# Sums of the stick-breaking attention: suffix sums of the key blocks on VectorE, a triangle and its complement on TensorE

## What is computed

```python
def block(args):
    qblk, qp = args
    z = jnp.einsum('bhqd,bhkd->bhqk', qblk, kh).astype(jnp.float32) * scale
    strict = kpos[None, :] < qp[:, None]
    log_beta = jax.nn.log_sigmoid(z)
    log_keep = jnp.where(strict, jax.nn.log_sigmoid(-z), 0.0)
    between = lax.cumsum(log_keep, axis=log_keep.ndim - 1, reverse=True) - log_keep
    w = jnp.where(strict, jnp.exp(log_beta + between), 0.0)
    return jnp.einsum('bhqk,bhkd->bhqd', w.astype(vh.dtype), vh)
```

## Time and profile before

| | us |
|---|---|
| time before, median of 3 runs | 2716.53 (2716.38 to 2717.42) |
| the profiled execution's own time | 2714.51 |
| its span | 2712.7 |
| TensorE busy | 2689.5 (99%) |
| VectorE busy | 1578.0 (58%) |
| ScalarE busy | 1152.4 (42%) |
| GpSimd busy | 625.4 (23%) |

### The profile page before, as it was taken

The page is one execution under the profiler, slowest core; times in us unless marked ns, Lnnn a source line. Parts: engine busy times, 40 slices in busy tenths (PEclk is TensorE's granted clock), DMA queues, the critical chain, the costliest instruction groups (busy, mean ns, idle before and its releaser), DMA issues.

```text
span 2712.7 us, 31969 instructions
## 1 busy us (share of the span) xinstructions
PE 2689.5 (99%) x12918; PEld 2252.7 (83%) x12918; DVE 1578.0 (58%) x2312; ACT 1152.4 (42%) x1836; POOL 625.4 (23%) x401
## 2 busy tenths in 40 slices
PE   8999999999999999999999999999999999999999
PEld 7888888888888888888888888788888888788887
DVE  6556555444566646665575678744545668755444
ACT  4323323222347636532236767522224667522223
POOL 1000111011136525400004642411102452411100
PEclk9999999999999999999999999999999999999999
DMA  4222232332221222223222221233233211233332
GB/s 161 96 100 93 95 104 93 101 100 95 90 80 56 72 70 67 90 97 101 93 95 94 78 70 32 81 98 101 94 98 101 77 62 48 70 100 95 95 99 79
DMA packets 69412, 238.78 MB, mean 88 GB/s; under 512 B 7696, under 2 KB 10256, under 8 KB 69264
## 3 DMA queue, kind: packets, MB, share of 16 engines
q1 hardware_dynamic: 69264, 236.73, 27.6%
HBM read 234.60 MB, written 2.10 MB: 87 GB/s over the span
## 4 chain that ended last, share of the span: by engine, by line
PE 93%; DVE 4%; ACT 2%; issue 0%; DMA 0%; POOL 0%; SPq 0%; ACTq 0%; DVEq 0%
PE ps L419 29%; PE ps L420 29%; PE ps L421 29%; DVE ptl L1569 1%; PE ps L555 1%; ACT wh L943 1%; PE ps L488 0%; PE ps L778 0%; PE ps L777 0%; PE ps L615 0%; PE ps L616 0%; PE ps L455 0%; ACT pth L952 0%; PE ps L474 0%; PE ps L479 0%
## 5 line engine op out<-in xcount | busy, mean ns | idle before, releaser
L943 ACT ACTIVATE wh<-raw 128x1024 fp32r<-128x1024 f32 (+2 forms) x453 | 464.7, 1027 | 731.3 <-PE ps L421 726.8
L419 PE MATMUL ps<-xh,wh 128*128 128x512 f32 x1920 | 751.5, 391 | 0.0
L421 PE MATMUL ps<-xh,wl 128*128 128x512 f32 x1920 | 747.4, 389 | 0.0
L420 PE MATMUL ps<-xl,wh 128*128 128x512 f32 x1920 | 747.3, 389 | 0.0
L1561 DVE TENSOR_TENSOR wl<-raw,wh 128x1024 fp32r<-128x1024 f32 (+1 forms) x339 | 448.9, 1325 | 148.6 <-ACT wh L943 148.4
L419 PE MATMUL ps<-yh,wh 128*128 128x512 f32 x1088 | 425.2, 391 | 2.6 <-ACT t L973 1.6
L420 PE MATMUL ps<-yl,wh 128*128 128x512 f32 x1088 | 423.4, 389 | 0.0
L421 PE MATMUL ps<-yh,wl 128*128 128x512 f32 x1088 | 423.4, 389 | 0.0
L419 PEld LDWEIGHTS ps<-xh,wh 128*128 128x128 f32 x1920 | 360.6, 188 | 75.5 <-issue 1.0
L421 PEld LDWEIGHTS ps<-xh,wl 128*128 128x128 f32 x1920 | 360.4, 188 | 75.2
L420 PEld LDWEIGHTS ps<-xl,wh 128*128 128x128 f32 x1920 | 360.6, 188 | 74.6 <-issue 1.0
(11 more groups left out here) (267 smaller groups left out, 3646.7 us busy)
## 6 DMA issues: line engine op xcount, KB each, us to landing
raw<-in_ff SPq DMA_DIRECT2D x120, 512.0 KB, 3.6
raw<-in_pool_in SPq DMA_DIRECT2D x64, 512.0 KB, 3.3
raw<-in_conv_in SPq DMA_DIRECT2D x64, 512.0 KB, 3.3
raw<-in_pool_out SPq DMA_DIRECT2D x32, 512.0 KB, 3.3
raw<-in_qk SPq DMA_DIRECT2D x32, 512.0 KB, 3.7
raw<-in_pool_grp SPq DMA_DIRECT2D x16, 512.0 KB, 3.3
raw<-in_conv_out SPq DMA_DIRECT2D x16, 512.0 KB, 3.3
raw<-in_mla_z SPq DMA_DIRECT2D x16, 512.0 KB, 3.6
```

What stands on the lines that cost most here:

```text
L419: pe.do.matmul(o, lh, rh_, start=start, stop=False)
L420: pe.do.matmul(o, lh, rl_, start=False, stop=False)
L421: return pe.do.matmul(o, ll, rh_, start=False, stop=stop)
L943: act.do.activation(h[:, 0:ncol], r[:, 0:ncol], ACT.Copy).then_inc(*mark("whi", ("whi", k)))
```

## The change

DVE's soft now forms suffix sums over the key blocks. Groups come in the order of blocks 2 and 3, block 1, block 0; behind each group one addition adds the next block's row to the queries that both have: block 3 to block 2 (128 columns), block 2 to block 1 (256), block 1 to block 0 (384). Each row of `SA` then holds the sum over its own block and all later ones. On PE a new constant `restr` is the complement of the triangle, ones minus `trir`. The triangle with a block's own suffix sum counts the later blocks in part, and the complement with the next block's suffix sum adds what is missing. So each key block needs two pairs instead of up to four, 7 pairs in all, 14 products. A group is `kept` only after its addition.

The two masks of blocks 2 and 3 become one product of 256 columns, with the mask read twice and two stretches of the bank written. The array of ones is no longer loaded; DVE makes it, and the sums of squares read it from `onesr` in full float32. They wait for DVE's start-up now instead of for the constants alone.

```diff
--- before.py
+++ after.py
@@ -43,9 +43,9 @@
 NVEC = _at
 
 
-C_ID, C_ONE, C_CAUS, C_CHUNK, C_INV, C_CNT, C_SGN, C_EPS = (
-    0, 128, 256, 384, 512, 513, 513 + 64, 513 + 65)
-NCONST = 513 + 66
+C_ID, C_CAUS, C_CHUNK, C_INV, C_CNT, C_SGN, C_EPS = (
+    0, 128, 256, 384, 385, 385 + 64, 385 + 65)
+NCONST = 385 + 66
 
 
 KOFF = (0, 512, 896, 1152)
@@ -315,6 +315,7 @@
         vec = sb("vec", NVEC)
         onesr = sb("onesr", 128, F32R)
         trir = sb("trir", 128, F32R)
+        restr = sb("restr", 128, F32R)
         identr = sb("identr", 128, F32R)
         hidden = sb("hidden", 128, F32R)
         small = sb("small", 64)
@@ -328,7 +329,7 @@
             return ap.bitcast(F32)
 
         ident = const[:, C_ID:C_ID + 128]
-        ones = const[:, C_ONE:C_ONE + 128]
+        ones = f(onesr[:, :])
         m_caus = const[:, C_CAUS:C_CAUS + 128]
         m_chunk = const[:, C_CHUNK:C_CHUNK + 128]
         m_before, m_after = OB[:, 0:128], OB[:, 128:256]
@@ -451,7 +452,7 @@
                         *mark("group", ("mm", "rs", use)))
                     return
                 pe.wait_ge(*at(*last_square(use)))
-                pe.wait_ge(*at("const"))
+                pe.wait_ge(*at("ones"))
                 pe.do.matmul(b[:, :], ones, ACC[:, :], start=True, stop=True).then_inc(
                     *mark("group", ("mm", "rs", use), ("accfree", use)))
 
@@ -758,24 +759,26 @@
                             mm3(o, k_h[rr, kc], k_l[rr, kc], q_h[rr, qc], q_l[rr, qc], kb == kbs[0], False)
                     for kbs, k0, width in GR:
                         b = ps("ss", l, h, kbs[0])
-                        for kb in kbs:
-                            o = b[:, KOFF[kb] - k0:KOFF[kb] - k0 + 128]
-                            mm = pe.do.matmul(o, identr[:, :], hidden[:, :], start=False, stop=kb == kbs[-1])
-                        mm.then_inc(*mark("group", ("mm", "ss", l, h, kbs[0])))
+                        o, cover = b[:, 0:128], hidden[:, :]
+                        if len(kbs) == 2:
+                            o = b[:, 0:512].rearrange("p (a c) -> p a c", a=2)[:, :, 0:128]
+                            cover = hidden[:, :].rearrange("p (a c) -> p a c", a=1).to_broadcast([128, 2, 128])
+                        pe.do.matmul(o, identr[:, :], cover, start=False, stop=True).then_inc(
+                            *mark("group", ("mm", "ss", l, h, kbs[0])))
 
                 def sb_between(h):
                     for n, (kbs, k0, width) in enumerate(GR):
-                        for jb in range(kbs[0], 4):
-                            pe.wait_ge(*at("kpl", l, h, {0: 0, 1: 1, 2: 2, 3: 2}[jb]))
+                        pe.wait_ge(*at("kpl", l, h, kbs[0]))
                         b = use(sb_banks[n], ("sb", l, h, kbs[0]))
                         for kb in reversed(kbs):
-                            for jb in range(kb, 4):
-                                lhs = trir if jb == kb else onesr
+                            for jb in range(kb, min(kb + 2, 4)):
+                                lhs = trir if jb == kb else restr
                                 c0 = KOFF[kb] - k0
                                 o = b[:, c0 + 128 * (jb - kb):c0 + 512 - 128 * kb]
                                 cc = slice(KOFF[jb], KOFF[jb] + 512 - 128 * jb)
                                 pe.do.matmul(o, lhs[:, :], SBH[:, cc], start=jb == kb, stop=False)
-                                mm = pe.do.matmul(o, lhs[:, :], SBL[:, cc], start=False, stop=jb == 3)
+                                mm = pe.do.matmul(o, lhs[:, :], SBL[:, cc], start=False,
+                                                  stop=jb == min(kb + 1, 3))
                         mm.then_inc(*mark("group", ("mm", "sb", l, h, kbs[0])))
 
                 def sb_pv(h):
@@ -1618,8 +1621,9 @@
                 weights(2)
                 dve.wait_ge(*at("const"))
                 dve.do.tensor_copy(identr[:, :], ident)
-                dve.do.tensor_copy(onesr[:, :], ones)
+                dve.do.tensor_scalar(onesr[:, :], ident, 0.0, 1.0, ALU.mult, ALU.add)
                 dve.do.tensor_copy(trir[:, :], m_after)
+                dve.do.tensor_tensor(restr[:, :], m_before, ident, ALU.add)
                 dve.do.tensor_scalar(hidden[:, :], m_before, 1.0, -NEG, ALU.subtract, ALU.mult).then_inc(
                     *mark("dve", ("ones",)))
 
@@ -2027,7 +2031,12 @@
                             *mark("dve"))
                         dve.wait_ge(*mine())
                         dve.do.scalar_tensor_tensor(a, src, 0.0, a, ALU.max, ALU.add).then_inc(
-                            *mark("dve", ("kept", l, h, kbs[0]), ("psfree", "ss", l, h, kbs[0])))
+                            *mark("dve", ("psfree", "ss", l, h, kbs[0])))
+                        kb = kbs[0]
+                        a = SA[:, KOFF[kb] + 128:KOFF[kb] + 512 - 128 * kb]
+                        dve.wait_ge(*mine())
+                        dve.do.tensor_tensor(a, a, SA[:, KOFF[kb + 1]:KOFF[kb + 1] + 384 - 128 * kb], ALU.add).then_inc(
+                            *mark("dve", ("kept", l, h, kb)))
 
                 def keep(h):
                     for kbs, k0, n in GR:
@@ -2633,7 +2642,6 @@
     p = np.arange(128)[:, None]
     n = np.arange(128)[None, :]
     c[:, C_ID:C_ID + 128] = p == n
-    c[:, C_ONE:C_ONE + 128] = 1.0
     c[:, C_CAUS:C_CAUS + 128] = np.where(n <= p, 0.0, NEG)
     c[:, C_CHUNK:C_CHUNK + 128] = np.where(n // 64 <= p // 64, 0.0, NEG)
     fr = np.arange(0, 64, 2, dtype=np.float32) / np.float32(64)
```

## The result

| | before | after |
|---|---|---|
| median of 10 runs each, us | 2715.57 (2713.76 to 2717.42) | 2725.11 (2721.02 to 2726.20) |
| profiled execution, us | 2714.51 | 2725.56 |
| its span, us | 2712.7 | 2723.8 |
| mean granted clock of its span | 1.000 | 0.994 |

The change makes the kernel 0.33% slower: ratio 1.0033, 95% interval 1.0024 to 1.0042. The forecast itself was 2719.5, and slower by 5.4 us or more had a chance of 0.22. As a difference the range was missed by a little: its upper end lay 9.0 us above the 2716.5 us that the prediction started from, and the change costs 9.5 us; the time is inside because the kernel before came out 1.0 us lower over ten runs.

The account below looks back on a forecast made before the run. TensorE, 99% busy, was taken as the bound, here and there just in time for DVE. Net +2.2 us for waits and +0.9 for POOL made +3.1, so 2716.5 became about 2719.5 us; range 2711 to 2725.5.

Parts of the forecast that it names:

- slower: Whole kernel: a measured time above 2722 us, some 5.4 us or more over the kernel before; chance 0.22.
- lost in 3: Head 3: PE waits at 2244.21 for a DVE chain begun before the sums, so the 0.58 us gain is lost.
- 1.33 us given back in 6 and 7: Heads 6 and 7: PE's waits at 2319.43 and 2330.87 move by the additions' 1.33 us each, swallowing the 0.58.
- heads 0, 1, 2 and 5 keep their 0.58: In these heads idle time of DVE hides the additions' 1.33 us, so shorter sums gain 0.58 us each.
- the lock on the shared port: Rival: additions in both heads 4 and head 0 of layer 0 wait out POOL; +9.6 us, 2726, chance 0.14.
- The +0.9 us that the prediction's sum had for POOL: Additions slowed beside POOL: 0.7 us in head 0 of layer 0, 0.1 in head 4 of each layer.
- all of this moves by 1.33 us, and the 0.58 is lost: Head 4: DVE is late, so PE's wait at 2265.18 for the last low half moves by 1.33 us.
- +2.2 for the waits: Both layers: per layer 2.87 us kept, 3.99 given back in heads 4, 6 and 7; net +2.2 us.
- queueing: Rival: heads 0 to 3 and 5 also pass on 1.33 us and lose 0.69; up to +20, 2740, chance 0.03.
- No new wait in heads 1, 2 and 5: Sign: PE's waits show none new in these heads, where the additions were taken as hidden.
- 2265 near 1.8: Sign: PE's wait at 2265 us, for the last low half of head 4, grows from 0.47 to near 1.8 us.
- Soft operations of 1.5 us and more in heads 4 to 7: Sign that the forecast is wrong towards slower: soft operations on DVE of such lengths beside POOL in these heads.

Follow-up runs that it names:

- e5: The changed kernel plus 26 useless constant products per layer on TensorE, in front of the five waits that grew: 2716.08 us, ratio 0.9998 to the kernel before.
- e2: Against the kernel before: masks merged, start-up changed, the additions in all heads, but the old 20 products per head (sums wrong): 2724.20 us, ratio 1.0028.
- e9: The changed kernel plus 4 useless products per layer at one place only, before the scores of head 4: 2724.82 us, ratio 1.0030 to the kernel before.
- e6: Against the kernel before: masks merged everywhere, additions and 14 products only in head 4 of layer 0 and head 3 of layer 1: 2717.54 us.
- e11: Control: the changed kernel plus 10 useless products per layer before proj(dk, 1), where TensorE does not wait: 2729.09 us, ratio 1.0049 to the kernel before.
- e7: Against the kernel before: masks merged everywhere, additions and 14 products only in head 6 of layer 0 and head 7 of layer 1: 2718.74 us.
- e8: Against the kernel before: masks merged everywhere, additions and 14 products only in heads 0, 1 and 5 of both layers: 2710.48 us, ratio 0.9979.

## Why the prediction was right and wrong

With e5 the forecast of the waits can be held against a clock that stays up. By how much the way from the first mask of one head to that of the next is longer (+) or shorter (-) than in the kernel before, layer 1, in us (difference of starts; the last row ends at sb_pv(7)):

| masks of head | predicted | e5_fill | after |
|---|---|---|---|
| 0 to 1 | -0.69 | -0.80 | -0.80 |
| 1 to 2 | -0.69 | -0.76 | -0.76 |
| 2 to 3 | -0.69 | +0.12 | +0.13 |
| 3 to 4 | -0.11 | -0.02 | +0.59 |
| 4 to 5 | +1.33 | -0.04 | +1.69 |
| 5 to 6 | -0.58 | -0.63 | -0.62 |
| 6 to 7 | -0.69 | -0.62 | -0.63 |
| 7 to end | +3.24 | +3.21 | +4.53 |
| sum | +1.12 | +0.46 | +4.13 |

**Right: prices and most places.** The sums of a head take 0.64 us less (2.08 for 2.71 in head 0), forecast 0.58. The additions take 0.29, 0.42 and 0.56 us where nothing disturbs them, forecast 0.28, 0.41 and 0.55 (timeline of DVE, head 6 of layer 1):

```profile
2313.50 0.29 DVE L2038 TENSOR_TENSOR s<-s 128x128 f32<-128x128 f32 x1
2314.89 0.42 DVE L2038 TENSOR_TENSOR s<-s 128x256 f32<-128x256 f32 x1
2316.68 0.56 DVE L2038 TENSOR_TENSOR s<-s 128x384 f32<-128x384 f32 x1
```

Heads 0, 1, 3, 5, 6 and 7 behave as forecast to about 0.1 us: gain kept in 0, 1 and 5, lost in 3, 1.33 us given back in 6 and 7. Head 6's wait was forecast near 2.3 and is 2.35, head 7's near 1.8 and is 1.92 in layer 0.

**Wrong: head 2.** The step "heads 0, 1, 2 and 5 keep their 0.58" fails here. Its additions meet GpSimd (layer 1, timelines of DVE and POOL):

```profile
2186.28 0.98 DVE L2038 TENSOR_TENSOR s<-s 128x128 f32<-128x128 f32 x1
2188.35 2.37 DVE L2038 TENSOR_TENSOR s<-s 128x256 f32<-128x256 f32 x1
...
2185.82 1.29 POOL L2375 TENSOR_TENSOR t<-t 128x512 f32<-128x512 f32 x1
2188.04 2.41 POOL L2352 TENSOR_TENSOR wl<-raw,wh 128x1024 fp32r<-128x1024 f32 x1 [0.93 <-ACT wh L946]
```

The second takes 2.37 us for 0.42. The prediction placed the lock on the shared port in head 4 and in head 0 of layer 0. In both layers the first two additions of head 2 and the last of head 3 meet it (2.08 us for 0.56):

```profile
2225.33 2.08 DVE L2038 TENSOR_TENSOR s<-s 128x384 f32<-128x384 f32 x1
```

In head 0 of layer 0 the second takes 1.46 for 0.42. All additions together take 15.5 and 14.4 us for 10.2 undisturbed, 9.5 us more over the kernel. The prediction let the lock decide for "slower" from 2.4 us of such stretching; it is four times that, and head 2 is the only place where it reaches PE, by 0.8 us a layer (+0.12 in the table for -0.69). The +0.9 us that the prediction's sum had for POOL, 0.7 in head 0 of layer 0 and 0.1 in each head 4, did not come: head 0 keeps its 0.80 us in both layers. By the Trainium skill, "SBUF — State Buffer", section "SBUF: two separate sides", whichever of the two engines starts first holds the port for its whole instruction; the trace agrees here: POOL started 0.31 us earlier and ends at 2190.45, the addition at 2190.72.

**Wrong: head 4.** The step "all of this moves by 1.33 us, and the 0.58 is lost" took from rows 7 that low halves take 1.62 us in heads other than 0. In head 4 they did not (before, timelines of DVE and POOL):

```profile
2260.24 4.89 DVE L1569 TENSOR_TENSOR ptl<-s,pth 128x384 fp32r<-128x384 f32 x3
...
2260.39 1.53 POOL L2366 TENSOR_TENSOR t<-t 128x512 f32<-128x512 f32 x1 [1.75 <-DVE t L1732]
2261.88 2.70 POOL L2343 TENSOR_TENSOR wl<-raw,wh 128x1024 fp32r<-128x1024 f32 x1
```

Of their 4.89 us some 3.3 are already the lock's. The same place in e5:

```profile
2260.15 1.61 DVE L1581 TENSOR_TENSOR ptl<-s,pth 128x384 fp32r<-128x384 f32 x3
...
2260.30 2.61 POOL L2384 TENSOR_TENSOR t<-t 128x512 f32<-128x512 f32 x1 [3.02 <-DVE t L1745]
```

Now the low halves take 1.61, and POOL waits (2.61 for 1.53). The lateness of 1.33 is paid out of the 3.3 us of lock that are no longer there, and PE is held next at the scores of differential head 3 instead. Which of the two starts first is not what differs: in both kernels POOL's product starts 0.15 us behind the first low half. Before, it gets in behind the first of the three, and the second and third wait for POOL; in e5 it waits for all three. The same two outcomes run through all fourteen traces, always with a distance of 0.15 or 0.16 us (once 0.06). Without additions in head 4 the three take 4.9 us, in all 17 cases (a case is one layer of one trace). With them they take 1.6 in seven cases (e2, e5 and e9 in both layers, e6 in layer 0) and 4.9 in four, the changed kernel (at 2267.15) and e11, and these four are those with a fall of 6.8 us just ahead. What turns it is not shown. A step beside a contested port can't be moved as a fixed length.

**The missing term: the clock.** "Granted clock full throughout" was read for the kernel before and taken as given for the changed one, while the same text forecast 13 us more idle time on TensorE. With what it brings along it costs 8.8 us in the profiled run (5.1 + 3.7) and 9.0 by the medians. Without it the forecast would have erred by less than its own margin: +3.1 in all, of which +2.2 for the waits, against +1.0 in e5. Part of that closeness is luck, since head 2 (+0.8 a layer) and head 4 (-1.4) err in opposite directions. And that the time lies inside the range at all is luck: a term that the sum did not have is three times the sum. Slower was priced by the port and by queueing alone (the port 2726, chance 0.14); the measured 2725.1 is near that number for another reason.

**Signs named beforehand.** Matmuls 112 fewer: yes. DVE 48 operations more and 20 us busier: 49 and 26. No new wait in heads 1, 2 and 5: not in 1 and 5; head 2 has one of 0.59. "2265 near 1.8" did not come; the waits moved to df_pv(2) and df_scores(3, 34). Idle time of PE up by 13 us: up by 10.3. Soft operations of 1.5 us and more in heads 4 to 7, the sign for "slower": none, and the kernel is slower all the same.

**Open.** What in detail lets the clock fall was not settled: e7 and e8 show that the last wait's length does not decide alone. And the 9 us hold what comes with the falls, the low halves of head 4 that wait for GpSimd again (4.89 us for 1.61) among it; the two were not taken apart. None of the traces is of a run of the kernel before at a clock of 0.998, so where its clock falls then is not known.

## What to carry to other kernels

When TensorE is 99% busy and work is taken off it at a place where another engine is just in time, the pauses that appear can have a second price beside their length: behind them TensorE may run at half clock, here about 9 us against 1 us of net waiting. Apply such a change only in the parts whose consumers have slack, which the timeline tells head by head; where a pause can't be avoided, cheap products on constants into the next bank kept the clock up here, when all five pauses were filled and not when one was. One profiled run that shows a full clock does not say that the kernel always has it: look at the clock of all runs. And a duration measured beside a contested port is not a property of the operation: it can turn out either way after the move, so run it.

## What was not expected of the hardware

Pauses of 0.95 to 2.6 us (in one run 0.29) on a TensorE that was otherwise busy were accompanied or followed by 3.4 to 10.2 us at half clock; 3.4 us of it cost 0.85 us in one place (e8) and 1.6 in another (e7). The falls come back in nearly the same places from kernel to kernel (1626, 1701, 2251, 2329), and filling one of them moves it on. The three low halves of head 4 took 4.89 us beside GpSimd, or 1.61, though GpSimd's product started 0.15 us behind the first of them in either case.
